# Feed-forward input products, tiles 2 to 10: weights stationary, tokens moving

## The chip, the cores and the metric

The kernel is one program on one core of a Trainium2 chip, one launch. The metric is the device time in microseconds, the median of a few runs; of the kernel before, three runs gave 1437.44 us (1437.07 to 1438.07).

## The reference

Two transformer-like blocks on 256 tokens of width 1024, in float32. The first has a recurrent and an attention branch. The second has two layers; each runs a feed-forward, a mixer, a second feed-forward and a gated embedding. There are thus four feed-forwards, and the change is in them:

```python
def swiglu(x, w_in, w_out):
    gate, up = jnp.split(x @ w_in, 2, axis=-1)
    return (jax.nn.silu(gate) * up) @ w_out

h = h + 0.5 * rmsnorm(swiglu(rmsnorm(h, g[0]), ffn1_w_in[i], ffn1_w_out[i]), g[1])
```

`w_in` is 1024 x 5632 and `w_out` 2816 x 1024. The norm ahead of `swiglu` divides each token by its root mean square; the kernel multiplies by the gains `g[0]` ahead of the products and by the token's scale behind them.

## The kernel before

**Products.** A float32 number is split into a high part, rounded to float32r, and the low part that is left. A product of two matrices is then three products of parts, high x high, high x low and low x high (`three`, lines 2113 to 2116); the product of the low parts is dropped.

**Weights.** All weights of the program are one list of units of 1 MB, 128 x 2048. Four slots hold the raw unit (`raw`), its high part (`whi`) and its low part (`wlo`). SyncE's queue loads a unit as soon as its raw slot is free. ScalarE makes the high part (`hi`, line 422; it waits until TensorE is done with the unit four before), VectorE the low part (`lo`, line 1202). Both work in a fixed order written out by hand for each engine, with their other steps between the units. The counters `n` hold which use of each semaphore is next.

**Tokens.** The 256 tokens are two blocks of 128. The input of a product stands transposed, features on partitions, in `feed_hi` and `feed_lo`. The 2816 features of the feed-forward are 11 tiles of 256; a unit pair holds the 256 gate and the 256 up columns of one tile, for the 1024 rows of depth. Tiles are worked on in pairs, a group of four units: `group_wide` on TensorE takes the tokens' first block through all four units into `acc[0]` and then the second block into `acc[1]`. A feed chunk of 128 x 128 (features x tokens of one block) is stationary and 512 columns of weights move, 12 products for a unit and a block. `acc[t]` is two PSUM banks, one for each tile of the pair. The last tile is alone.

**Behind the products.** When `acc[t]` is complete, ScalarE takes silu of the gate columns, scaled by `pre_rs` (the token's 1/rms, one number for each partition), into `sgl` (line 676), and VectorE multiplies the up columns, `pre_rs` and `sgl` into `hid` and frees `acc[t]` (`mul`, line 1707). Tokens lie on partitions in `hid`, and the output product needs features there, so TensorE turns it: four transposes of 128 x 128 into a bank of `turn` (`hidden`, line 2400, and `turns`, line 2167). ScalarE copies the high part to `hid_hi` (line 683) and VectorE the low part to `hid_lo` (line 1716). Each `hidden` is a hook put into the stream of products of the block after: in the loop, the turn of the pair's second block is done before the last unit of the next group's first block.

**Around the loop.** The first group has hooks of its own: the turn of the normed input's second block, and `hidden(0, 0)` before the third unit of its second block. Then comes a loop of four groups (tiles 2 to 9), tile 10 alone, and the output products in `group_deep` (groups of 3, 4 and 4 units), whose first units carry the last turns. In ScalarE's and VectorE's order, the high and low part of the first group's last slot (unit 7 counted from the start of the feed-forward) come before silu and `mul` of that group's second block.

Of the kernel before, what the change touches and what calls it, by code (L numbers as in the profile page):

```python
# [20 lines left out]
F32 = mybir.dt.float32  # L21
F32R = mybir.dt.float32r
# [4 lines left out]
P = 128  # L27
SEQ, D = 256, 1024
# [16 lines left out]
FF_GROUPS = FF_TILES // 2  # L45
# [69 lines left out]
def build(nc, io):  # L115
    with ExitStack() as ctx:
        def sem(name):
            return ctx.enter_context(nc.semaphore(name))
# [19 lines left out]
        feed_hi = sb("feed_hi", [P, KC, SEQ], F32R)  # L138
        feed_lo = sb("feed_lo", [P, KC, SEQ], F32R)
# [100 lines left out]
        gains2 = sb("gains2", [P, D])  # L240
        assert base[0] <= pp1_at
# [119 lines left out]

        ple_gate, ple_mul, ple_hi, ple_lo = sem("ple_gate"), sem("ple_mul"), sem("ple_hi"), sem("ple_lo")
# [29 lines left out]

        def chunks(ap, n=4):
            return [ap[:, P * i:P * i + P] for i in range(n)]
# [10 lines left out]
        def _(act):  # L405
            n = {"u": 0, "e": [0, 0], "first": 0, "used": 0, "tb": 0, "ss": 0, "h": 0, "ple": 0, "mix": 0, "pre": 0}
# [266 lines left out]
            def ffn(second, layer):  # L673
# [5 lines left out]
                def hidden(g, t, count=4, it=None):  # L679
                    b = next_turn(it)  # L680
                    dst = hid_hi[:, 4 * g:4 * g + count, lanes(t)] if it is None else \
                        hid_hi[:, bass.ds(it * 4 + 4 * g, 4), lanes(t)]
                    act.activation(dst, turn[:, b, 0:P * count].rearrange("p (c s) -> p c s", c=count),  # L683
                                   ACT.Copy).then_inc(fed_hi, 1)

# [33 lines left out]
                hidden(0, 0)  # L719
# [4 lines left out]
                loops = FF_GROUPS - 1  # L724
                start = {k: list(v) if k == "e" else v for k, v in n.items()}
                with act.Fori(0, FF_GROUPS - 1) as it:
                    hidden(0, 1, it=it)
                    silu(0, it)
                    hi(3, it)
                    hidden(1, 0, it=it)  # L730
                    hi(1, it)
                    silu(1, it)
                n.update(u=start["u"] + RING * loops, used=start["used"] + RING * loops,
                         first=start["first"] + loops, tb=start["tb"] + 2 * loops,
                         e=[k + loops for k in start["e"]])

                sums(0)
                act.activation(sgl[:, 0, 0, :], acc[0][:, 0:256], ACT.Silu, scale=pre_rs[:, 0:1]).then_inc(silu_done, 1)
                hi()
                sums(1, units=2)  # L740
                act.activation(sgl[:, 1, 0, :], acc[1][:, 0:256], ACT.Silu, scale=pre_rs[:, 1:2]).then_inc(silu_done, 1)
                hidden(FF_GROUPS - 1, 1)
                hi(3)
                hidden(FF_GROUPS, 0, 2)
                hi()
                hidden(FF_GROUPS, 1, 2)
                if not second and layer == 0:
                    embed(0)
                hi(2 * RING - 4)
# [431 lines left out]
        def _(dve):  # L1181
            n = {"u": 0, "e": [0, 0], "first": 0, "used": 0, "tb": 0, "fed": 0, "rs": 0, "step": 0, "silu": 0,
                 "h": 0, "ple": 0, "post": 0, "pre": 0, "aux": 0, "att": 0}
# [516 lines left out]
            def ffn(second, layer):  # L1700
                def mul(t, it=None, tiles=2, units=RING):

                    no_sums(t, units)
                    n["silu"] += 1
                    dve.wait_ge(silu_done, n["silu"] if it is None else it * 2 + n["silu"])
                    up = acc[t][:, :].rearrange("p (i n) -> p i n", i=2)[:, 0:tiles, 256:512]
                    dve.scalar_tensor_tensor(hid[:, t, 0:tiles, :], up, pre_rs[:, t:t + 1], sgl[:, t, 0:tiles, :],  # L1707
                                             ALU.mult, ALU.mult)\
                        .then_inc(acc_free[t], 1)

                def hidden(g, t, count=4, it=None):
                    b = next_turn(it)
                    n["fed"] += 1
                    dve.wait_ge(fed_hi, n["fed"] if it is None else it * 2 + n["fed"])
                    at = slice(4 * g, 4 * g + count) if it is None else bass.ds(it * 4 + 4 * g, 4)
                    dve.tensor_tensor(hid_lo[:, at, lanes(t)],  # L1716
                                      turn[:, b, 0:P * count].rearrange("p (c s) -> p c s", c=count),
                                      hid_hi[:, at, lanes(t)].bitcast(F32), ALU.subtract).then_inc(moved[b], 1)
# [8 lines left out]
                hidden(0, 0)  # L1727
                lo()
                mul(1)
                loops = FF_GROUPS - 1  # L1730
                start = {k: list(v) if k == "e" else v for k, v in n.items()}
                with dve.Fori(0, loops) as it:
                    hidden(0, 1, it=it)
                    mul(0, it)
                    lo(3, it)
                    hidden(1, 0, it=it)
                    lo(1, it)
                    mul(1, it)
                n.update(u=start["u"] + RING * loops, used=start["used"] + RING * loops,
                         first=start["first"] + loops, tb=start["tb"] + 2 * loops, fed=start["fed"] + 2 * loops,  # L1740
                         silu=start["silu"] + 2 * loops, e=[k + loops for k in start["e"]])
                mul(0, tiles=1)
                lo()
                mul(1, tiles=1, units=2)
                hidden(FF_GROUPS - 1, 1)
                lo()
                lo(2)
                hidden(FF_GROUPS, 0, 2)
                lo()
                hidden(FF_GROUPS, 1, 2)  # L1750
                if not second and layer == 0:
                    embed(0)
                lo(2 * RING - 4)
# [93 lines left out]
            def even():  # L1847
# [6 lines left out]
                assert turns0 % 2 == 0  # L1854
# [249 lines left out]
        def _(pe):  # L2104
            n = {"u": 0, "e": [0, 0], "tb": 0, "h": 0, "dve": 0, "act": 0, "aux": 0, "normed": 0}
# [293 lines left out]
            def ffn(second, layer):  # L2399
                def hidden(g, t, count=4, it=None, back=0):  # L2400

                    pe.wait_ge(acc_free[t], n["e"][t] - back if it is None else it + n["e"][t])
                    turns([hid[:, t, c // 2, P * (c % 2):P * (c % 2) + P] for c in range(count)], it)

                all_moved()
                group_wide(["wide"] * 4, [lambda: feed_normed(xn[:, 1, :]), lambda: hidden(0, 0),
                                          all_moved])
                loops = FF_GROUPS - 1
                start = {k: list(v) if k == "e" else v for k, v in n.items()}
                with pe.Fori(0, loops) as it:  # L2410
                    group_wide(["wide"] * 4, [lambda: hidden(0, 1, it=it), lambda: hidden(1, 0, it=it), None], it)
                n.update(u=start["u"] + RING * loops, tb=start["tb"] + 2 * loops, e=[k + loops for k in start["e"]])
                group_wide(["wide"] * 2, [lambda: None, lambda: hidden(FF_GROUPS - 1, 1, back=1), None])

                hooks = [lambda: hidden(FF_GROUPS, 0, 2, back=1), lambda: hidden(FF_GROUPS, 1, 2, back=1), None]
                group_deep(3, hid_hi, hid_lo, 0, True, False, hooks)
# [423 lines left out]
```

## Time and profile before

| | |
|---|---|
| median of three runs | 1437.44 us |
| the profiled execution | 1437.7 us |
| its span, first to last instruction | 1435.8 us |
| TensorE busy | 1411.9 us, 98% |
| VectorE busy | 874.5 us, 61% |
| ScalarE busy | 710.2 us, 49% |
| mean granted TensorE clock | 0.999 |
| DMA | 272.5 MB, mean 190 GB/s |

Busy time of TensorE counts each matmul from its start to its modelled end, and these overlap, so it says that TensorE always had something in hand and not that it ran at its peak. The time that one instruction costs is read from start to start in the timeline. A line of the program is often that of a helper: L2114, L2115 and L2116 are the three products of `three`, L2167 is the transpose, L422 and L1202 the high and low part of a unit. In the rows, 128x512 is partitions x elements; PE is TensorE, PEld its weight loads, DVE VectorE, ACT ScalarE, POOL GpSimd.

### The profile page before, as it was taken

How to read it: one execution, taken by the hardware profiler on the slowest of the kernel's cores; microseconds unless marked ns; L12 is line 12 of the kernel's file. 1: busy time of each engine (PE TensorE's matmuls, PEld its weight loads, DVE VectorE, ACT ScalarE, POOL GpSimd, SP SyncE). 2: the span in 40 equal slices, each digit the busy share in tenths (PEclk: the TensorE clock that was granted, in tenths of full speed). 3: DMA queues.
4: the chain of work that ended last, by engine and by line, in shares of the span. 5: the costliest groups of instructions: out<-in, count | busy, mean ns of one | idle time of the engine just before them, and what ended most of it. 6: DMA issues, size and time to landing. Idle time of an engine off the chain costs nothing.

```text
span 1435.8 us, 17115 instructions
## 1 busy us (share of the span) xinstructions
PE 1411.9 (98%) x6598; PEld 1168.0 (81%) x6598; DVE 874.5 (61%) x813; ACT 710.2 (49%) x723; POOL 75.4 (5%) x91
## 2 busy tenths in 40 slices
PE   7999999999999999999999999999999999999997
PEld 6888888878888888888888878888888878888886
DVE  6869686775463666774544684544774546554536
ACT  4674766545343557654443554443544445353424
POOL 0000000010000200110000110000202101000001
PEclk9999999999999999999999999999999999999999
DMA  9747554465464453464645374645463633654541
GB/s 393 296 150 264 179 178 168 164 243 207 172 217 163 179 210 118 147 226 155 234 176 196 142 263 148 234 176 203 155 228 118 221 131 139 228 188 163 201 181 44
DMA packets 40380, 272.51 MB, mean 190 GB/s; under 512 B 4609, under 2 KB 5505, under 8 KB 8706
## 3 DMA queue, kind: packets, MB, share of 16 engines
q1 hardware_dynamic: 36864, 261.65, 50.2%
q10 hardware_dynamic: 3458, 10.04, 2.0%
q8 instruction: 42, 0.69, 0.2%
q14 instruction: 16, 0.13, 0.0%
HBM read 270.62 MB, written 1.05 MB: 189 GB/s over the span
## 4 chain that ended last, share of the span: by engine, by line
PE 91%; DVE 4%; DMA 3%; ACT 1%; issue 1%; POOL 1%; SPq 0%; ACTq 0%; DVEq 0%; POOLq 0%
PE acc L2114 28%; PE acc L2116 28%; PE acc L2115 28%; PE turn L2167 4%; DVE wlo L1202 2%; DMA raw<-in_units 2%; DMA mod_raw<-in_units 1%; PE aux L2654 0%; PE turn L2316 0%; PE aux L2528 0%; DMA gpost<-in_g_final 0%; DVE h L1272 0%; ACT whi L422 0%; DVE xn L1256 0%; DVE mod_part L1321 0%
## 5 line engine op out<-in xcount | busy, mean ns | idle before, releaser
L1202 DVE TENSOR_TENSOR wlo<-raw,whi 128x2048 fp32r<-128x2048 f32 x233 | 533.1, 2297 | 257.4 <-ACT whi L422 257.3
L2114 PE MATMUL acc<-whi,feed_hi 128*128 128x512 f32 (+1 forms) x1496 | 595.1, 398 | 4.2 <-DVE wlo L1202 4.2
L2116 PE MATMUL acc<-whi,feed_lo 128*128 128x512 f32 (+1 forms) x1496 | 582.6, 389 | 0.0
L2115 PE MATMUL acc<-wlo,feed_hi 128*128 128x512 f32 (+1 forms) x1496 | 581.9, 389 | 0.0
L422 ACT ACTIVATE whi<-raw 128x2048 fp32r<-128x2048 f32 x233 | 445.3, 1917 | 255.8 <-PE acc L2116 243.5
L2114 PEld LDWEIGHTS acc<-whi,feed_hi 128*128 128x128 f32 x1496 | 281.7, 188 | 65.1 <-DVE wlo L1202 6.5
L2116 PEld LDWEIGHTS acc<-whi,feed_lo 128*128 128x128 f32 x1496 | 281.3, 188 | 59.6
L2115 PEld LDWEIGHTS acc<-wlo,feed_hi 128*128 128x128 f32 x1496 | 281.8, 188 | 55.7 <-issue 1.2
L2114 PE MATMUL acc<-whi,hid_hi 128*128 128x512 f32 x352 | 138.0, 392 | 0.0
L2116 PE MATMUL acc<-whi,hid_lo 128*128 128x512 f32 x352 | 137.1, 389 | 0.0
L2115 PE MATMUL acc<-wlo,hid_hi 128*128 128x512 f32 x352 | 137.0, 389 | 0.0
L2116 PEld LDWEIGHTS acc<-whi,hid_lo 128*128 128x128 f32 x352 | 66.1, 188 | 13.7
L2115 PEld LDWEIGHTS acc<-wlo,hid_hi 128*128 128x128 f32 x352 | 66.1, 188 | 13.4
L2114 PEld LDWEIGHTS acc<-whi,hid_hi 128*128 128x128 f32 x352 | 66.1, 188 | 13.3
L683 ACT ACTIVATE hid_hi<-turn 128x512 f32 (+2 forms) x48 | 26.4, 550 | 99.3 <-PE turn L2167 99.3
L1716 DVE TENSOR_TENSOR hid_lo<-turn,hid_hi 128x512 f32 (+2 forms) x48 | 30.8, 642 | 71.8 <-ACT hid_hi L683 71.8
L1102 POOL TENSOR_SCALAR ms<-ss 128x1 f32<-128x1 f32 x18 | 12.2, 680 | 1033.7 <-ACT xn L442 1011.4
L1707 DVE SCALAR_TENSOR_TENSOR hid<-acc,pre_rs,sgl 128x512 f32<-128x512 f32 (+1 forms) x48 | 33.8, 704 | 44.0 <-ACT sgl L676 40.1
L464 ACT ACTIVATE feed_hi<-turn 128x512 fp32r<-128x512 f32 x48 | 26.2, 594 | 56.4 <-PE turn L2167 56.4
L1240 DVE TENSOR_TENSOR feed_lo<-turn,feed_hi 128x512 fp32r<-128x512 f32 x48 | 30.9, 684 | 30.7 <-ACT feed_hi L464 30.7
L676 ACT ACTIVATE sgl<-acc,pre_rs 128x512 f32<-128x512 f32 x40 | 27.2, 679 | 37.1 <-PE acc L2116 37.1
L1265 DVE SCALAR_TENSOR_TENSOR xn<-acc,gpost 128x1024 f32<-128x1024 f32 x12 | 14.6, 1221 | 38.4 <-ACT xn L442 38.4
(338 smaller groups left out, 879.7 us busy)
## 6 DMA issues: line engine op xcount, KB each, us to landing
raw<-in_units SPq DMA_DIRECT2D x237, 1024.0 KB, 4.9
mod_raw<-in_units SPq DMA_DIRECT2D x6, 1024.0 KB, 11.2
gpost<-in_norm_g ACTq DMA_DIRECT2D x8, 512.0 KB, 4.8
gpre<-in_norm_g ACTq DMA_DIRECT2D x6, 512.0 KB, 5.7
mod_more<-in_units SPq DMA_DIRECT2D x2, 1024.0 KB, 23.5
h<-in_x SPq DMA_DIRECT2D x2, 512.0 KB, 10.6
w_ax<-in_w_ax SPq DMA_DIRECT2D x1, 1024.0 KB, 26.2
bgate<-in_b_gate SPq DMA_DIRECT2D x1, 1024.0 KB, 27.5
```

The source lines that it names most:

```text
L422: act.activation(whi[:, u % RING, :], raw[:, u % RING, :], ACT.Copy).then_inc(hi_ready, 1)
L464: act.activation(dst[:, 4 * i:4 * i + 4, lanes(t)], turn[:, b, :].rearrange("p (c s) -> p c s", c=4), ACT.Copy).then_inc(fed_hi, 1)
L676: act.activation(sgl[:, t, :, :], acc[t][:, :].rearrange("p (i n) -> p i n", i=2)[:, :, 0:256], ACT.Silu, scale=pre_rs[:, t:t + 1]).then_i ...
L683: act.activation(dst, turn[:, b, 0:P * count].rearrange("p (c s) -> p c s", c=count), ACT.Copy).then_inc(fed_hi, 1)
L1202: dve.tensor_tensor(wlo[:, u % RING, :], raw[:, u % RING, :], whi[:, u % RING, :].bitcast(F32), ALU.subtract).then_inc(lo_ready, 1)
L1240: dve.tensor_tensor(dst[part], turn[:, b, :].rearrange("p (c s) -> p c s", c=4), hi_part[part].bitcast(F32), ALU.subtract).then_inc(moved[ ...
L1707: dve.scalar_tensor_tensor(hid[:, t, 0:tiles, :], up, pre_rs[:, t:t + 1], sgl[:, t, 0:tiles, :], ALU.mult, ALU.mult)\
L1716: dve.tensor_tensor(hid_lo[:, at, lanes(t)], turn[:, b, 0:P * count].rearrange("p (c s) -> p c s", c=count), hid_hi[:, at, lanes(t)].bitca ...
L2114: pe.matmul(out, xh, wh, start=first, stop=False)
L2115: pe.matmul(out, xh, wl, start=False, stop=False)
L2116: return pe.matmul(out, xl, wh, start=False, stop=last)
L2167: last = pe.transpose(turn[:, b, P * i:P * i + P], part, ident[:, :])
```

## The change

Tiles 0 and 1 stay as they were. For tiles 2 to 10 the roles are exchanged: a block of 128 x 128 weights is stationary and the tokens move. `feed_hi` and `feed_lo` are now two halves of one tensor `feeds`, so that one matmul of 512 columns takes the high weights through both, and one of 256 columns takes the low weights through the high feed. The result has 128 features on partitions and, for each of two banks (0 gate, 1 up), high-feed sums in the columns 0 to 255 and low-feed sums in 256 to 511. `acc[c]` holds the feature block c of the tile; it gets two units of products, and not four.

The two halves of a bank are added by two engines: ScalarE copies the second half to `sgl` (`tile_rest`), VectorE adds the first (`tile_sum`) and frees `acc[c]`. The token scale now differs along the free dimension, so it is turned once for each feed-forward into a row `rs_row` that stands on all partitions (`rows_scale` on TensorE, a copy on VectorE), and VectorE multiplies all four sums by it (`tile_scale`). ScalarE takes silu, VectorE the product, ScalarE the high part and VectorE the low part, all in SBUF. There are no transposes for these tiles; `hid_split` counts them for TensorE ahead of the output products. `hidden(1)`, the turn of the first group's second block, now stands between the first and second unit of tile 2's block c = 0. The program runs tile 2, a loop of 3 x 2 tiles, and tiles 9 and 10.

```diff
@@ allocation @@
-        feed_hi = sb("feed_hi", [P, KC, SEQ], F32R)
-        feed_lo = sb("feed_lo", [P, KC, SEQ], F32R)
+        feeds = sb("feeds", [P, 2, KC, SEQ], F32R)
+        feed_hi, feed_lo = feeds[:, 0, :, :], feeds[:, 1, :, :]
...
+        rs_row = sb("rs_row", [P, SEQ])
@@ ScalarE @@
+                def tile_gate(it=None):
+                    n["scaled"] += 1
+                    act.wait_ge(gate_scaled, n["scaled"] if it is None else it * 2 + n["scaled"])
+                    act.activation(sgl[:, :, 0, :], sgl[:, :, 0, :], ACT.Silu).then_inc(silu_done, 1)
+
+                def tile_rest(c, it=None):
...
+                    both = acc[c][:, :].rearrange("p (i x n) -> p i x n", i=2, x=2)
+                    act.activation(sgl[:, c, :, :], both[:, :, 1, :], ACT.Copy).then_inc(rest_copied, 1)
+
+                def tile_hi(j, it=None):
...
+                    act.activation(hid_hi[:, at, :], hid[:, :, 0, :], ACT.Copy).then_inc(fed_hi, 1)
+
+                def tile_done(j, it=None):
+                    hi(1, it)
+                    tile_rest(1, it)
+                    hi(1, it)
+                    tile_gate(it)
+                    tile_hi(j, it)
+                    if j < FF_LAST:
+                        tile_rest(0, it)
...
                 hi(3)
-                hidden(0, 0)
+                n["tb"] += 1
+                hidden(0)
                 hi()
                 if late:
                     pre_scale(1)
                 silu(1)
...
+                hidden(1)
+                tile_rest(0)
+                tile_done(FF_FIRST)
...
+                with act.Fori(0, FF_LOOPS) as it:
+                    for j in (FF_FIRST + 1, FF_FIRST + 2):
+                        tile_done(j, it)
@@ VectorE @@
+                def tile_sum(c, it=None):
...
+                    dve.tensor_tensor(sgl[:, c, :, :], both[:, :, 0, :], sgl[:, c, :, :], ALU.add).then_inc(acc_free[c], 1)
+
+                def tile_scale(it=None):
+
+                    for c in range(2):
+                        dve.wait_ge(acc_free[c], n["e"][c] if it is None else it * 2 + n["e"][c])
+                    rows = sgl[:, :, :, :].rearrange("p t i n -> p (t i) n")
+                    dve.tensor_tensor(rows, rows, rs_row[:, :].rearrange("p (o n) -> p o n", o=1)
+                                      .to_broadcast([P, 4, SEQ]), ALU.mult).then_inc(gate_scaled, 1)
+
+                def tile_product(it=None):
...
+                    dve.tensor_tensor(hid[:, :, 0, :], sgl[:, :, 0, :], sgl[:, :, 1, :], ALU.mult).then_inc(hid_made, 1)
+                    n["made"] += 1
+                    dve.wait_ge(hid_made, n["made"] if it is None else it * 2 + n["made"])
+
+                def tile_lo(j, it=None):
...
+                    dve.tensor_tensor(hid_lo[:, at, :], hid[:, :, 0, :], hid_hi[:, at, :].bitcast(F32), ALU.subtract)\
+                        .then_inc(hid_split, 1)
+
+                def tile_done(j, it=None):
+                    tile_sum(1, it)
+                    tile_scale(it)
+                    lo(1, it)
+                    tile_product(it)
+                    if j < FF_LAST:
+                        tile_sum(0, it)
+                    tile_lo(j, it)
+                    lo(1, it)
...
                 mul(0)
                 lo(3)
-                hidden(0, 0)
+                row_moved = take(rs_row[:, :], columns=SEQ, groups=1)
+                hidden(0)
                 lo()
                 mul(1)
...
+                hidden(1)
+                dve.wait_ge(moved[row_moved[0]], row_moved[1])
+                tile_sum(0)
+                tile_done(FF_FIRST)
@@ TensorE @@
+                def hidden(t):
+
+                    pe.wait_ge(acc_free[t], n["e"][t])
+                    turns([hid[:, t, c // 2, P * (c % 2):P * (c % 2) + P] for c in range(4)])
+
+                def rows_scale():
+                    pe.wait_ge(pre_rstd, TOK * ((1, 3), (4, 6))[layer][1 if second else 0])
+                    turns([pre_rs[:, t:t + 1].to_broadcast([P, P]) for t in range(TOK)])
+
+                def turned_unit(u, half, c):
+
+                    s = u % RING
+                    for b in range(2):
+                        both = acc[c][:, BANK * b:BANK * b + BANK]
+                        for k in range(4):
+                            kc, at = 4 * half + k, BANK * k + SEQ * b + P * c
+                            w = slice(at, at + P)
+                            pe.matmul(both, whi[:, s, w], feeds[:, :, kc, :], start=kc == 0, stop=False)
+                            ins = pe.matmul(both[:, 0:SEQ], wlo[:, s, w], feed_hi[:, kc, :], start=False, stop=kc == KC - 1)
+                    return ins
+
+                def tile(it=None, hook=None):
+
+                    u0 = n["u"]
+                    n["u"] += 2
+                    for c in range(2):
+                        ready(c, None if it is None else it * 2)
+                        for half in range(2):
+                            if half and not c and hook is not None:
+                                hook()
+                            unit(u0 + half, c, it)
+                            ends(turned_unit(u0 + half, half, c), c, half == 1)
...
+                def second_hook():
+                    rows_scale()
+                    hidden(0)
+
+                group_wide(["wide"] * 4, [lambda: feed_normed(xn[:, 1, :]), second_hook, all_moved])
+                tile(hook=lambda: hidden(1))
+                tile()
...
+                with pe.Fori(0, FF_LOOPS) as it:
+                    for _ in range(2):
+                        tile(it)
...
+                tile()
+
+                all_moved()
...
+                pe.wait_ge(hid_split, split0 + 7 - FF_FIRST)
+                group_deep(3, hid_hi, hid_lo, 0, True, False, [None, None, None])
                 group_deep(4, hid_hi, hid_lo, 6, False, False, [None, None, None])
-                all_moved()
+                pe.wait_ge(hid_split, n["split"])
```

## Rows read from the trace of the kernel before

**Rows 1.** The page: busy time by engine, then the chain that ended last.
```profile
PE 1411.9 (98%) x6598; PEld 1168.0 (81%) x6598; DVE 874.5 (61%) x813; ACT 710.2 (49%) x723; POOL 75.4 (5%) x91
...
PE 91%; DVE 4%; DMA 3%; ACT 1%; issue 1%; POOL 1%; SPq 0%; ACTq 0%; DVEq 0%; POOLq 0%
PE acc L2114 28%; PE acc L2116 28%; PE acc L2115 28%; PE turn L2167 4%; DVE wlo L1202 2%; DMA raw<-in_units 2%; DMA mod_raw<-in_units 1%; PE aux L2654 0%; PE turn L2316 0%; PE aux L2528 0%; DMA gpost<-in_g_final 0%; DVE h L1272 0%; ACT whi L422 0%; DVE xn L1256 0%; DVE mod_part L1321 0%
```

**Rows 2.** Timeline inside a feed-forward (start, us, engine, line, operation): products, one turn.
```profile
700.13 0.39 PE L2116 MATMUL acc<-whi,feed_lo 128*128 128x512 f32 x1
...
702.85 0.39 PE L2116 MATMUL acc<-whi,feed_lo 128*128 128x512 f32 x1
...
703.09 0.60 PE L2167 MATMUL turn<-setup,hid 128*128 128x128 f32 x4
...
703.44 0.48 PE L2114 MATMUL acc<-whi,feed_hi 128*128 128x512 f32 x1
...
703.75 0.40 PE L2115 MATMUL acc<-wlo,feed_hi 128*128 128x512 f32 x1
```

**Rows 3.** Timeline of TensorE, third feed-forward: group 2, first output product, a small turn.
```profile
855.49 0.39 PE L2114 MATMUL acc<-whi,feed_hi 128*128 128x512 f32 x1
...
957.78 0.39 PE L2114 MATMUL acc<-whi,hid_hi 128*128 128x512 f32 x1
...
962.99 0.39 PE L2116 MATMUL acc<-whi,hid_lo 128*128 128x512 f32 x1
...
963.67 0.39 PE L2115 MATMUL acc<-wlo,hid_hi 128*128 128x512 f32 x1
```

**Rows 4.** Timeline of TensorE in the even mixer: first and last of 24 narrow products.
```profile
504.10 0.28 PE L2114 MATMUL acc<-whi,feed_hi 128*128 128x256 f32 x1
...
506.85 0.28 PE L2116 MATMUL acc<-whi,feed_lo 128*128 128x256 f32 x1
```

**Rows 5.** Timeline of VectorE, then of ScalarE, where the third feed-forward enters group 2.
```profile
854.98 2.29 DVE L1202 TENSOR_TENSOR wlo<-raw,whi 128x2048 fp32r<-128x2048 f32 x1 [0.92 <-ACT whi L422]
...
857.19 0.68 DVE L1716 TENSOR_TENSOR hid_lo<-turn,hid_hi 128x512 fp32r<-128x512 f32 x1
857.79 2.28 DVE L1202 TENSOR_TENSOR wlo<-raw,whi 128x2048 fp32r<-128x2048 f32 x1
859.99 0.74 DVE L1707 SCALAR_TENSOR_TENSOR hid<-acc,pre_rs,sgl 128x512 f32<-128x512 f32 x1
...
855.75 1.92 ACT L422 ACTIVATE whi<-raw 128x2048 fp32r<-128x2048 f32 x1 [0.32 <-PE acc L2116]
```

**Rows 6.** Timeline where a turn waits for VectorE, before the third feed-forward.
```profile
825.12 0.69 DVE L1256 TENSOR_TENSOR xn<-h,gpre 128x512 f32<-128x512 f32 x1
...
825.87 0.66 PE L2167 MATMUL turn<-setup,xn 128*128 128x128 f32 x4 [0.73 <-DVE xn L1256]
...
826.28 0.48 PE L2114 MATMUL acc<-whi,feed_hi 128*128 128x512 f32 x1
...
826.60 0.40 PE L2115 MATMUL acc<-wlo,feed_hi 128*128 128x512 f32 x1
```

**Rows 7.** Groups by line and shape, whole run: busy, mean ns, idle before.
```profile
L1240 DVE TENSOR_TENSOR feed_lo<-turn,feed_hi 128x512 fp32r<-128x512 f32 x48 | 30.9, 684 | 30.7 <-ACT feed_hi L464 30.7
...
L1716 DVE TENSOR_TENSOR hid_lo<-turn,hid_hi 128x256 fp32r<-128x256 f32 x8 | 3.3, 418 | 0.0
...
L1779 DVE TENSOR_TENSOR xn<-xn,pp 128x1024 f32<-128x1024 f32 x2 | 2.4, 1222 | 2.7 <-ACT xn L781 2.7
...
L676 ACT ACTIVATE sgl<-acc,pre_rs 128x512 f32<-128x512 f32 x40 | 27.2, 679 | 37.1 <-PE acc L2116 37.1
...
L524 ACT ACTIVATE xn<-acc 128x512 f32<-128x512 f32 x4 | 2.4, 590 | 5.2 <-PE acc L2116 5.2
```

**Rows 8.** Stretches: us, busy time of five engines, granted clock, DMA.
```profile
14.00:18.00 4.00, 1.09 (x6) 0.69 (x5) 3.89 (x5) 1.15 (x2) 0.09 (x1) 1.00 1.01 420
...
1434.00:1436.00 2.00, 0.00 (x0) 0.00 (x0) 0.00 (x0) 0.00 (x0) 0.00 (x0) 0.50 0.46 170
```

More of the change, by code:

```diff
@@ L1700, in ffn, with mul @@
             def ffn(second, layer):
-                def mul(t, it=None, tiles=2, units=RING):
-                    no_sums(t, units)
+                def mul(t):
+                    no_sums(t)
+                    n["silu"] += 1
+                    dve.wait_ge(silu_done, n["silu"])
+                    up = by_two(acc[t][:, :])[:, :, 256:512]
+                    dve.scalar_tensor_tensor(hid[:, t, :, :], up, pre_rs[:, t:t + 1], sgl[:, t, :, :],
+                                             ALU.mult, ALU.mult)\
+                        .then_inc(acc_free[t], 1)
@@ new lines, in hidden @@
+                def hidden(t):
+                    b = next_turn()
+                    n["fed"] += 1
+                    dve.wait_ge(fed_hi, n["fed"])
+                    dve.tensor_tensor(hid_lo[:, 0:4, lanes(t)], turn[:, b, :].rearrange("p (c s) -> p c s", c=4),
+                                      hid_hi[:, 0:4, lanes(t)].bitcast(F32), ALU.subtract).then_inc(moved[b], 1)
+                def tile_sum(c, it=None):
+                    no_sums(c, 2)
+                    both = acc[c][:, :].rearrange("p (i x n) -> p i x n", i=2, x=2)
+                    n["rest"] += 1
+                    dve.wait_ge(rest_copied, n["rest"] if it is None else it * 4 + n["rest"])
+                    dve.tensor_tensor(sgl[:, c, :, :], both[:, :, 0, :], sgl[:, c, :, :], ALU.add).then_inc(acc_free[c], 1)
@@ L1726, in ffn @@
                 lo(3)
-                hidden(0, 0)
+                row_moved = take(rs_row[:, :], columns=SEQ, groups=1)
+                hidden(0)
                 lo()
                 mul(1)
-                loops = FF_GROUPS - 1
+                hidden(1)
+                dve.wait_ge(moved[row_moved[0]], row_moved[1])
+                tile_sum(0)
+                tile_done(FF_FIRST)
                 start = {k: list(v) if k == "e" else v for k, v in n.items()}
[L1732 to L1750, printed above, removed]
+                with dve.Fori(0, FF_LOOPS) as it:
+                    for j in (FF_FIRST + 1, FF_FIRST + 2):
+                        tile_done(j, it)
+                n.update(u=start["u"] + RING * FF_LOOPS, used=start["used"] + RING * FF_LOOPS,
+                         first=start["first"] + 2 * FF_LOOPS, fed=start["fed"] + 2 * FF_LOOPS,
+                         silu=start["silu"] + 2 * FF_LOOPS, e=[k + 2 * FF_LOOPS for k in start["e"]],
+                         made=start["made"] + 2 * FF_LOOPS, rest=start["rest"] + 4 * FF_LOOPS)
+                tile_done(FF_LAST - 1)
+                tile_done(FF_LAST)
+                lo(3)
                 if not second and layer == 0:
                     embed(0)
-                lo(2 * RING - 4)
+                lo()
+                lo(3)
                 for t in range(TOK):
```

88 lines of the change are left out of this document (35 added, 53 removed).

## The prediction

> **What bounds the kernel now.** I read the page first: TensorE is busy 98% of the span, the chain that ended last is 91% TensorE, and the lines of the weight products (28% each) carry it [rows 1]. A busy TensorE row proves little, since each matmul record lasts 0.39 us while the next starts 0.227 us later, so I went to the timeline and read start to start. Twelve steps from 700.13 to 702.85 give 0.2267 us for a matmul of 512 columns, and nothing stands between them: in this stage TensorE streams without a wait, and an edit is worth what it changes in the number and width of TensorE's instructions, plus any wait that it creates. All four feed-forwards have the same steps, so I work one out and take it four times. In the third, the second group (feature tiles 2 and 3) starts at 855.49 and the first product of the output matrix at 957.78: 102.29 us for tiles 2 to 10 [rows 3].
>
> **Price of a turn.** Four transposes between products: from the product at 702.85 to the third after it (703.75) are 0.90 us, less two steps of 0.2267, so 0.447 us [rows 2]. A turn of two: 962.99 to 963.67 is 0.68, less 0.453, so 0.227 us [rows 3].
>
> **Width.** In the 256-column products of the even mixer, 23 steps take 506.85 - 504.10 = 2.75 us, so 0.1196 each [rows 4]. That is 0.1071 less than at 512 columns, which is 256 columns at 2.4 GHz; what is left of either step (0.2267 - 0.2133, 0.1196 - 0.1067) is a fixed 13 ns per product. Every product here loads its own weights, at both widths, so the load is already inside the step.
>
> **Products, removed and added.** A tile before: 2 blocks of tokens x 8 chunks of depth x 3 products x 512 columns = 48 steps. After: 4 feature blocks x 8 chunks x (one of 512, both feeds together, and one of 256) = 32 + 32 steps. The columns are the same, 24,576; there are 16 more instructions at 13 ns, +0.21 us a tile. With the units' edges included: 102.29 less 9 full turns (4.02) over 4x96 + 48 = 432 products is 0.2275 us a step, and 0.2275 - 0.1071 = 0.1204 for the narrow one. Nine tiles: 288 x 0.2275 + 288 x 0.1204 = 65.5 + 34.7 = 100.2 us.
> The moving operand is now two runs of 256 from two feeds. No row shows such a read. Below, it costs nothing (one run of 512 [rows 2]); above, what two separate products cost more than one, 2 x 0.1196 - 0.2267 = 0.0125 us each, 1152 of them, 14.4 us. I take nothing, since the number of columns streamed is the same; the upper end stays for the range.
> The Trainium skill (TensorE: Matmul & The Clock Gate, "Back-to-back issue gap") puts a single gap at N/2.4 plus 2.5 ns. By it the 16 extra products of a tile would cost 0.04 us and not 0.21, and the sum for four feed-forwards would be 6 us lower. Rows 2 and 4 disagree, with 13 ns at both widths; the measurement decides.
>
> **Turns, removed and added.** After 855.49 the old code has 9 full turns and 2 small ones (those fall into the first output products). The new one has one full turn, `hidden(1)`, and one of two transposes, the scale row, directly ahead of the turn of `hidden(0)`; next to another turn it costs about the difference between full and small spread over two transposes more, (0.447 - 0.227)/4 x 2 = 0.11; with a wait of its own I take 0.14 us.
>
> **The new wait.** `hidden(1)` stood before the last unit of the next block, 36 products or 8.2 us into group 2. It now stands after the first half of tile 2's first block: 8 x (0.2275 + 0.1204) = 2.78 us after 855.49. It waits for `acc_free[1]`, that is for VectorE's `mul(1)`, which VectorE does only after the low part of unit 7. That unit's slot comes free when the group ends: ScalarE starts its copy at 855.75, VectorE subtracts from 857.79, and `mul(1)` runs from 859.99 to 860.73 = 5.24 us after the group's start [rows 5]. Before, this was 3 us early; now it is late. In front of it VectorE gets one more instruction, the copy of the scale row out of PSUM, 128x256, 0.42 us by the 128x256 row [rows 7]: the feed part (857.19) shifts to about 857.53, unit 7 from 857.79 to 858.13, so `mul(1)` ends 0.34 later, at 5.58. A turn released by VectorE starts 0.06 us after it (825.12 + 0.69 = 825.81, turn at 825.87) and then takes 0.41 + 0.32 instead of 0.35 + 0.31 to the second product, 0.07 more [rows 6]. Stall: 5.64 - 2.78 + 0.07 = 2.9 us. Behind the turn in TensorE's queue wait all products of tile 2, so nothing hides it. Bounds: 2.6 (the copy fits into a gap) to 3.6 us (a wait's hand-over of 0.3 twice). The copies of ScalarE and VectorE are one tile ahead of need, so nothing is won back.
>
> **Is the rest covered?** Per tile of 32 x 0.3479 = 11.13 us, by durations of [rows 5, 7] and counted from the end of a tile's second block: ScalarE copies half of `acc[1]` 0.26 to 0.85, VectorE adds to 1.57, scales (128x1024, 1.22) to 2.85, low part of the next unit to 5.1, product to 5.8; ScalarE the high part of hid to 6.4, the copy from `acc[0]` to 7.0; VectorE its sum to 7.7, low part of hid 8.4, second unit 10.7. TensorE needs `acc[1]` at 5.5 (has it at 1.6) and `acc[0]` at 11.1 (7.7); VectorE is through 1.3 us ahead of its next sum (12.0). VectorE does 2 x 0.68 + 1.22 + 2 x 0.69 [rows 6] + 2 x 2.29 = 8.5 of 11.1 us. The edit costs nothing there as long as this slack lasts. Loads: the number and order of units is the same; SyncE's queue sees the slots come free singly and not in threes.
> The thinnest place is the entry to the output matrix: its third unit is needed after 24 steps, 5.46 us, and has its low part at 5.1. Cover 0.3 us; I take no stall, and 0.3 us x 4 as the upper end.
>
> **Sum.** One feed-forward before: 102.29 + 2 x 0.227 = 102.74. After: 100.18 + 0.45 + 0.14 + 2.9 = 103.7. Difference +0.95, of which the turns give -4.0, the extra instructions +1.9, the copy of the scale row's turn +0.14 and the stall +2.9. Four times: +3.8 us. The profiled execution took 1437.7 us (span 1435.8), which gives 1441.5; from the median of 1437.44 it is 1441.2 us.
>
> **Rivals.**
> *No stall, faster.* If the wait at half a tile is met in time, the turns removed win: 4 x (0.95 - 2.9) = -7.8, 1429.6 us. For it: the turns are worth 4 us in each feed-forward. Against: the chain 0.26 + 1.92 + 2.29 + 0.74 after the group's end is all serial and its records [rows 5] end at 5.24; it decides at 2.78. Chance 0.10, which includes a lower fixed cost of a product than I read.
> *Clock.* TensorE has no record for about 2.8 us in each stall. In the stretch 14 to 18 us it sat idle 2.9 us at a granted clock of 1.00; after the last product the clock is 0.50 [rows 8]. If it fell to 1.2 GHz for as long as the stall, 2.9 us of work would take twice that: 4 x 2.9/2 = +5.8, 1447 us. Chance 0.10. The Trainium skill (same page, "Why this matters for your kernels") warns against idle gaps between bursts for this reason; the nearest row has a gap of this size without it.
> *Vector chain late.* If VectorE's tile takes longer than 11.13 (waits for its own results, the in-place sum in strided halves), each tile is late by the excess: 0.3 us x 36 = +10.8, 1452 us. For it: five hand-overs a tile between two engines, four more than before. Against: 1.3 us of slack. Chance 0.10.
> *Narrow products cost more.* If a weight load of 0.19 us were exposed under a 256-column product, 1152 x 0.07 = +80, 1518 us. The even mixer's rows [rows 4] are exactly such products at 0.1196. Chance 0.03; a few ns for the split read fall into the range instead.
>
> **How the numbers follow.** The forecast holds 0.67 by itself. A change under 0.2% (2.9 us) can't be told from none. The forecast's +3.8 lies 0.9 above that; with its own scatter of about 1.5 us a quarter of it, 0.17, lies within. Slower 0.50 + 0.10 + 0.10 + 0.03 = 0.73; same 0.17; faster 0.10. The range runs from 1437.6 (stall at its lower end and half the extra instructions free) to 1450 (the clock case, and most of a late vector chain or of the split read).
>
> **What would show it.** After: no turn between products from tile 3 on; steps of 0.227 and 0.120 in turn; a tile period of 11.1 us; one gap ahead of the turn in tile 2 of each feed-forward, released by VectorE's `mul`, 2.9 us long; output products starting 103.5 us after tile 2 does; no wait at `acc_free` or a unit's low part elsewhere; granted clock 1.00. Wrong if that gap is missing or shorter than 2 us, if a pair of steps isn't 0.347, or if gaps recur tile by tile.

## The result and the profile after

The changed kernel takes 1448.54 us (median of 5 runs, 1447.81 to 1451.84) against 1437.31: ratio 1.0083, 95% interval 1.0072 to 1.0095. It is slower by 11.2 us, where +3.8 was forecast; the time lies inside the range of 1437.6 to 1450 and on the side that was forecast, but the size was a third of what came. The profiled execution took 1447.81 us, its span is 1446.0, 10.2 us over the span before.

The page of the changed kernel; the first two lines answer to [rows 1], the others are the new products (busy, mean ns).

```profile
PE 1412.0 (98%) x7038; PEld 1187.3 (82%) x7038; DVE 959.4 (66%) x917; ACT 748.6 (52%) x787; POOL 75.2 (5%) x91
...
PE 89%; DVE 6%; DMA 2%; ACT 2%; issue 1%; POOL 1%; SPq 0%; ACTq 0%; DVEq 0%; POOLq 0%
...
L2484 PE MATMUL acc<-feeds,whi 128*128 128x512 f32 x1152 | 406.5, 397 | 0.0
...
L2485 PE MATMUL acc<-feeds,wlo 128*128 128x256 f32 x1152 | 323.9, 281 | 0.0
```

TensorE is as busy as before by the page, and its busy time is the same; neither tells of the 10 us. VectorE's share of the chain rose from 4 to 6%, since the chain now runs through VectorE's work ahead of each new wait. The timeline shows the wait. VectorE, then TensorE, in the third feed-forward, where tile 2 starts at 859.76 (this answers to [rows 5]):

```profile
861.46 0.42 DVE L1262 COPY rs_row<-turn 128x256 f32<-128x256 f32 x1
861.79 0.68 DVE L1748 TENSOR_TENSOR hid_lo<-turn,hid_hi 128x512 fp32r<-128x512 f32 x1
862.39 2.28 DVE L1235 TENSOR_TENSOR wlo<-raw,whi 128x2048 fp32r<-128x2048 f32 x1
864.59 0.75 DVE L1740 SCALAR_TENSOR_TENSOR hid<-acc,pre_rs,sgl 128x512 f32<-128x512 f32 x1
...
862.45 0.28 PE L2485 MATMUL acc<-feeds,wlo 128*128 128x256 f32 x1
865.39 0.66 PE L2234 MATMUL turn<-setup,hid 128*128 128x128 f32 x4 [2.66 <-DVE hid L1740]
865.80 0.48 PE L2484 MATMUL acc<-feeds,whi 128*128 128x512 f32 x1
...
867.04 0.63 PE L2484 MATMUL acc<-feeds,whi 128*128 128x512 f32 x1
867.47 0.41 PE L2485 MATMUL acc<-feeds,wlo 128*128 128x256 f32 x1
867.68 0.63 PE L2484 MATMUL acc<-feeds,whi 128*128 128x512 f32 x1
```

`mul(1)` ends at 865.34, 5.58 us after the tile's start, to the hundredth as worked out. The last product before the turn starts at 862.45 and the turn at 865.39, 2.94 us later in place of 0.12: the stall. Behind it the products first go on at their old step, and then take 0.43 and 0.21 us in place of 0.23 and 0.12. The stretches of the same trace (us, five engines, granted clock, DMA) say why:

```profile
862.60:865.30 2.70, 0.13 (x2) 0.00 (x0) 2.70 (x2) 0.00 (x0) 0.00 (x0) 1.00 0.87 309
865.30:870.30 5.00, 4.91 (x21) 4.29 (x22) 0.73 (x2) 0.60 (x1) 0.00 (x0) 0.66 0.66 256
870.30:875.30 5.00, 5.00 (x30) 4.35 (x30) 0.69 (x1) 2.51 (x2) 0.00 (x0) 1.00 0.00 0
```

The mean of 0.66 is a mixture of the two levels: behind the stall the clock was at 1.2 GHz for a part of these 5 us, while TensorE worked through them. The same happened at all four stalls of this execution, and the granted clock of the five runs (0.994, 0.994, 0.994, 0.996 and 0.995, against 0.998 to 0.999 of the kernel before) says that none of them was free of it.

There is a third thing, in no view by groups. Eleven products of 512 columns and ten of 256, in the first and in the third feed-forward, far from any stall and at a granted clock of 1.00:

```profile
350.20 0.39 PE L2484 MATMUL acc<-feeds,whi 128*128 128x512 f32 x1
...
353.67 0.39 PE L2484 MATMUL acc<-feeds,whi 128*128 128x512 f32 x1
...
880.12 0.40 PE L2484 MATMUL acc<-feeds,whi 128*128 128x512 f32 x1
...
883.65 0.40 PE L2484 MATMUL acc<-feeds,whi 128*128 128x512 f32 x1
```

A pair is one wide product and the narrow one behind it. Ten pairs take 3.47 us in the one and 3.53 in the other. Over the last 256 pairs the mean is 0.3467 us in three feed-forwards and 0.3533 in the third, without exception inside a feed-forward: behind the stall and the lowered clock it is in one step or the other to its end. Ahead of the turn all four are alike, at 0.351 (seven pairs from 859.76 to 862.22). The 288 pairs of nine tiles take 99.8 or 101.75 us.

The account by feed-forward, from tile 2's start to the first output product (before: 102.29, and two small turns of 0.227 behind it, so 102.74):

| | measured | pairs | turn, stall | left: lower clock |
|---|---|---|---|---|
| first | 104.47 | 99.84 | 3.35 | 1.3 |
| second | 104.59 | 99.84 | 3.35 | 1.4 |
| third | 106.57 | 101.75 | 3.35 | 1.5 |
| fourth | 104.65 | 99.84 | 3.35 | 1.5 |

The last column is what the other two leave of the measured time. The sum is 420.3 against 411.0, +9.3. The first group, which now holds the turn of the scale row, takes 0.17, 0.21, 0.20 and 0.24 us more than before, +0.8 (worked out: 0.6), and 0.1 is spread over the rest.

### The profile page after: what moved, and what is told of

It is laid out like the page before. It is cut to its first block, busy times and chain, and to the rows that moved or that the text cites. A ratio compares the mean times of both kernels' runs of the same rounds, so it can differ in the third digit from the quotient of the medians.

```text
span 1446.0 us, 18169 instructions
## 1 busy us (share of the span) xinstructions
PE 1412.0 (98%) x7038; PEld 1187.3 (82%) x7038; DVE 959.4 (66%) x917; ACT 748.6 (52%) x787; POOL 75.2 (5%) x91
## 4 chain that ended last, share of the span: by engine, by line
PE 89%; DVE 6%; DMA 2%; ACT 2%; issue 1%; POOL 1%; SPq 0%; ACTq 0%; DVEq 0%; POOLq 0%
PE acc L2181 18%; PE acc L2484 18%; PE acc L2183 18%; PE acc L2182 18%; PE acc L2485 9%; DVE wlo L1235 3%; PE turn L2234 3%; ACT whi L431 1%; DMA mod_raw<-in_units 1%; DMA gpost<-in_norm_g 1%; PE aux L2758 0%; PE turn L2383 0%; PE aux L2309 0%; PE aux L2632 0%; DMA gpost<-in_g_final 0%
## 5 line engine op out<-in xcount | busy, mean ns | idle before, releaser
L2484 PE MATMUL acc<-feeds,whi 128*128 128x512 f32 x1152 | 406.5, 397 | 0.0
L2181 PE MATMUL acc<-whi,feeds 128*128 128x512 f32 (+1 forms) x888 | 354.5, 399 | 4.2 <-DVE wlo L1235 4.2
L2183 PE MATMUL acc<-whi,feeds 128*128 128x512 f32 (+1 forms) x888 | 345.8, 389 | 0.0
L2182 PE MATMUL acc<-wlo,feeds 128*128 128x512 f32 (+1 forms) x888 | 345.2, 389 | 0.0
L2485 PE MATMUL acc<-feeds,wlo 128*128 128x256 f32 x1152 | 323.9, 281 | 0.0
L2484 PEld LDWEIGHTS acc<-feeds,whi 128*128 128x128 f32 x1152 | 218.3, 190 | 50.4
L2485 PEld LDWEIGHTS acc<-feeds,wlo 128*128 128x128 f32 x1152 | 219.5, 191 | 0.2
L2181 PEld LDWEIGHTS acc<-whi,feeds 128*128 128x128 f32 x888 | 167.6, 189 | 41.9 <-DVE wlo L1235 6.8
L2183 PEld LDWEIGHTS acc<-whi,feeds 128*128 128x128 f32 x888 | 167.3, 188 | 35.4
L2182 PEld LDWEIGHTS acc<-wlo,feeds 128*128 128x128 f32 x888 | 167.7, 189 | 32.8 <-issue 0.7
L1757 DVE TENSOR_TENSOR sgl<-acc,sgl 128x512 f32<-128x512 f32 x72 | 49.8, 692 | 122.4 <-ACT sgl L708 122.4
L708 ACT ACTIVATE sgl<-acc 128x512 f32<-128x512 f32 x72 | 42.5, 590 | 43.5 <-PE acc L2485 43.5
```

The lines of the kernel that those rows point to most:

```text
L708: act.activation(sgl[:, c, :, :], both[:, :, 1, :], ACT.Copy).then_inc(rest_copied, 1)
L1757: dve.tensor_tensor(sgl[:, c, :, :], both[:, :, 0, :], sgl[:, c, :, :], ALU.add).then_inc(acc_free[c], 1)
L2181: pe.matmul(out, xh, wh, start=first, stop=False)
L2182: pe.matmul(out, xh, wl, start=False, stop=False)
L2183: return pe.matmul(out, xl, wh, start=False, stop=last)
L2484: pe.matmul(both, whi[:, s, w], feeds[:, :, kc, :], start=kc == 0, stop=False)
```

## Experiments

Each is timed against the kernel before on the same chip, 1437.3 us in the first two sets and 1437.5 in the last. "The nine tiles" is the time from tile 2 to the first output product.

**e1_hook_late.** The turn later; `hidden(1)` behind `tile_rest(0)` and `tile_sum(0)` on the other engines.

```diff
-                            if half and not c and hook is not None:
+                            if half and c and hook is not None:
...
-                tile(hook=lambda: hidden(1))
+                tile(hook=lambda: hidden(1, back=1))
```

> The changed kernel, with one turn moved: hidden(1) stands before the last half of tile 2's second block, 8.3 us into the tile and not 2.8, by when VectorE's mul has freed the bank (5.6 us). ScalarE's and VectorE's work on the tile's first block goes ahead of their part of the turn. Theory (the stall and the clock that falls behind it are the whole loss): no gap and granted clock 1.00; per feed-forward -4.03 us of turns, +1.57 us for the 16 more products a tile (9 tiles, 0.3467 us a pair as measured), +0.2 for the scale row's turn: 4 x -2.3 = -9 us against before, about 1428. Rival (the products themselves are dearer, the stall was hidden elsewhere): 1437 or more. If the gap goes but the clock still falls: about 1434.

Measured: 1436.09 us, ratio 0.9989 (0.9980 to 0.9999). No gap, clock 1.00, nine tiles in 102.24, 102.23, 102.24 and 102.22 us. The stall and the fallen clock are gone and the time is 12.4 us less; but all four feed-forwards run at 0.3533 us a pair, which is 7.6 us over an expectation that had taken 0.3467 for all. The theory was right about what the stall costs and wrong that nothing else was left.

**e2_mul_early.** The same end by the other side of the wait.

```diff
-                hi()
                 if late:
                     pre_scale(1)
                 silu(1)
+                hi()
 ...
                 lo(3)
+                mul(1)
                 row_moved = take(rs_row[:, :], columns=SEQ, groups=1)
                 hidden(0)
                 lo()
-                mul(1)
```

> The changed kernel with the turn where the change put it, but silu(1) and mul(1) put ahead of the high and low part of unit 7, in ScalarE's and VectorE's order. Theory: mul(1) ends 2.5 us after tile 2's start and the turn is asked for at 2.78, so the gap closes to under 0.3 us and the clock stays: about 1428 us, as with the later turn. Rival (the gap is set by another wait, such as the buffer of the turn): the gap stays at 2.8 us and the time at 1448. Second rival (moving the low part of unit 7 back by 0.75 us makes TensorE wait for it in tile 3): a new wait on L1235, 1430 or more.

Measured: 1436.39 us (1432.61 to 1436.96, 10 runs), ratio 0.9991 (0.9982 to 1.0001). The gap is gone. Timeline where it was, VectorE's `mul` and TensorE's turn, which starts 0.22 us after the last product:

```profile
334.47 0.75 DVE L1740 SCALAR_TENSOR_TENSOR hid<-acc,pre_rs,sgl 128x512 f32<-128x512 f32 x1
...
335.47 0.28 PE L2485 MATMUL acc<-feeds,wlo 128*128 128x256 f32 x1
...
335.69 0.63 PE L2234 MATMUL turn<-setup,hid 128*128 128x128 f32 x4
```

The time is 8 us over the 1428 that was expected. No new wait on unit 7 appears. The nine tiles take 102.32, 100.46, 102.32 and 100.47 us: two feed-forwards in the slow step and two in the fast. That profile is of the fastest run; the others lie at 1434.5, 1434.9, 1435.3 and 1436.2 to 1437.0, which fits up to two slow steps (1.9 us each) above; their granted clock is the same, 0.998 to 0.999. So one kernel changes its step from run to run: this is read from the times, since only one run has a trace.

**e3_fill_stall.** Work in the stall.

```diff
+                def filled():
...
+                    for _ in range(11):
+                        pe.matmul(turn[:, b, :], feed_hi[:, 0, 0:P], feeds[:, :, 0, :], start=True, stop=True)
+                    hidden(1)
...
+                tile(hook=filled)
```

> The changed kernel, with 11 matmuls of 512 columns put into each stall, ahead of the wait; their sums go to the buffer of the turn and are overwritten by it. The wait is as long, but TensorE works 2.5 of its 2.8 us. Theory (the clock falls because TensorE is idle in the stall): the turn starts at the same time after tile 2's start (5.6 us), granted clock 1.00 behind it, and 1.3 to 1.5 us less in each feed-forward than in the changed kernel, 5.7 us or more in all: 1441 to 1443. Rival (the slow steps behind the stall come from the layout or from the restart): they stay, 1448.

Measured: 1447.19 us (1445.33 to 1447.50, 4 runs). The timeline around the first stall: the turn comes when VectorE is done, as ever, and behind it stand steps of 0.31 and 0.12, not 0.58 and 0.21.

```profile
335.48 2.72 PE L2511 MATMUL turn<-feeds 128*128 128x512 f32 x11
...
338.30 0.66 PE L2234 MATMUL turn<-setup,hid 128*128 128x128 f32 x4
...
338.72 0.48 PE L2484 MATMUL acc<-feeds,whi 128*128 128x512 f32 x1
...
339.03 0.28 PE L2485 MATMUL acc<-feeds,wlo 128*128 128x256 f32 x1
...
339.15 0.40 PE L2484 MATMUL acc<-feeds,whi 128*128 128x512 f32 x1
```

The clock was 1.00 behind all four. The time missed the forecast because all four feed-forwards are at 0.3533: 101.75 + 0.45 + 2.9 = 105.1, measured 105.06 each. What the clock gave back (5.6 us) the step took (5.7 us, three more slow ones). A trace without a fall could be luck, as e7's below; but the other three runs show 0.998 to 0.999 as well, so of 16 filled stalls few or none had a fall, against 0.994 to 0.996 in every run of the changed kernel. Without the trace this run would have spoken against the right cause.

**e4_before_early_hook.** The kernel before, with the wait at the wrong place.

```diff
+                if it is not None and t == 0:
+                    return i == 1
```

> The kernel before, without the change, but in its loop the turn of a pair's second block stands before the second unit of the next group and not before the fourth, 2.73 us after the group's start. VectorE's mul ends 5.24 us after it. 16 stalls in all. Theory (wait alone): each is 5.24 + 0.06 - 2.73 + 0.07 = 2.6 us, +42 us, 1479.6. With the clock falling behind each as in the changed kernel (1.3 to 1.7 us): +63 to +70, 1500 to 1507. Rival (the clock falls for what is special in the changed kernel): 1480.

Measured: 1498.54 us, +61.2. There are 16 gaps of 2.82 to 2.89 us between starts. Behind 12 of them the clock fell, each time at a loss of about 1.6 us, and behind 4 not. Two gaps of the same length, one with and one without:

```profile
365.38 0.66 PE L2167 MATMUL turn<-setup,hid 128*128 128x128 f32 x4 [2.44 <-DVE hid L1707]
...
366.81 0.63 PE L2115 MATMUL acc<-wlo,feed_hi 128*128 128x512 f32 x1
367.23 0.63 PE L2116 MATMUL acc<-whi,feed_lo 128*128 128x512 f32 x1
...
392.37 0.65 PE L2167 MATMUL turn<-setup,hid 128*128 128x128 f32 x4 [2.44 <-DVE hid L1707]
...
393.56 0.39 PE L2114 MATMUL acc<-whi,feed_hi 128*128 128x512 f32 x1
393.79 0.39 PE L2115 MATMUL acc<-wlo,feed_hi 128*128 128x512 f32 x1
```

16 x 2.67 + 12 x 1.6 = 61.9, where the nine tiles of the four feed-forwards are longer by 62.0. So both prices belong to the wait, not to the new layout, and the layout before had them as well once its hook asked too early. The Trainium skill (TensorE: Matmul & The Clock Gate, "Why this matters for your kernels") advises against idle gaps between bursts of matmuls, naming longer ones than these. The traces agree in kind, with a fall behind 12 of 16 gaps here and at 4 of 4 in the changed kernel, and show that it is not certain: 4 of 16 went without one here, and all 4 in e7's trace below.

**e5_grouped_early, e7_grouped_only.** Four wide products and then four narrow ones, without and with the stall.

```diff
                         for k in range(4):
                             ...
                             pe.matmul(both, whi[:, s, w], feeds[:, :, kc, :], start=kc == 0, stop=False)
+                        for k in range(4):
+                            ...
                             ins = pe.matmul(both[:, 0:SEQ], wlo[:, s, w], feed_hi[:, kc, :], start=False, stop=kc == KC - 1)
```

> As e2_mul_early (no stall), and in each bank the four products of 512 columns of a unit come first and then the four of 256, in place of wide and narrow in turn. The same 64 products a tile. In the runs so far a pair in turn takes 0.3467 us in some feed-forwards and 0.3533 in others, 1.9 us for each that is in the slow step. Theory (the two steps come from wide and narrow in turn): eight products take 4 x 0.2267 + 4 x 0.1196 = 1.385 us in every feed-forward, and the time is that of e2 with no slow one, 1428 to 1430 us, with less spread than e2's 4 us. Rival (the slow step comes from the weights as stationary operand or from the two feeds read as one operand): the spread stays and the median is 1436.

Measured: 1433.34 us (1433.00 to 1434.12, 8 runs), ratio 0.9973 (0.9962 to 0.9983); nine tiles in 101.62, 101.62, 101.61 and 101.61 us. The timeline, two rounds of a bank:

```profile
701.12 1.09 PE L2484 MATMUL acc<-feeds,whi 128*128 128x512 f32 x4
702.05 0.64 PE L2488 MATMUL acc<-feeds,wlo 128*128 128x256 f32 x4
702.52 1.09 PE L2484 MATMUL acc<-feeds,whi 128*128 128x512 f32 x4
```

Over the last 256 pairs, eight products take 1.403 us, 0.3508 a pair, and not the 1.385 that I had added up, which is why the time is 3 us over the expected range. The steps of 0.3467 and 0.3533 are gone, the spread with them (1.1 us for 4.4), so it is the alternation that lets them lie 1.9 us a feed-forward apart; the level is between the two.

> The changed kernel with its stall, and the grouped order of e5_grouped_early. Theory: stall of 2.9 us and fallen clock stay (1.3 to 1.7 us a feed-forward), the slow step goes: per feed-forward 99.8 + 0.45 + 2.9 + 1.4 = 104.5, against 104.5 to 106.6 in the changed kernel, so 1445.5 to 1447 us with little spread, against 1447.8 to 1451.8. Rival: the spread and the median of 1448.5 stay.

Measured: 1446.79 us (1444.60 to 1450.52, 4 runs). The spread stayed, against what I expected, but it is now of the clock alone. The profiled execution is the fastest, and in it the clock fell behind none of four stalls (nine tiles: 104.33 to 104.36, where 101.0 + 0.45 + 2.9 = 104.4). The runs of 1444.60, 1445.71, 1447.87 and 1450.52 us have granted clocks of 0.999, 0.998, 0.996 and 0.994: the time grows as the clock falls, and the slowest, 5.9 us or four times 1.5 longer, has the clock of the changed kernel with four falls. The same order of products with the same stall thus has anything from no fall to about four.

**e6_feeds_adjacent, e9_flip_every_chunk.** Two more tries at the step.

```diff
-        feeds = sb("feeds", [P, 2, KC, SEQ], F32R)
+        feeds = sb("feeds", [P, KC, 2, SEQ], F32R)
...
-                            pe.matmul(both, whi[:, s, w], feeds[:, :, kc, :], start=kc == 0, stop=False)
+                            pe.matmul(both, whi[:, s, w], feeds[:, kc, :, :], start=kc == 0, stop=False)
```

> As e2_mul_early, but the two feeds of a depth chunk lie side by side in SBUF, so that the moving operand of 512 columns is one run and not two of 256. Theory (the split read costs nothing and has no part in the two steps): both steps again, 0.3467 and 0.3533, median 1432 to 1437. Rival (the split read makes the slow step): 0.3467 everywhere, 1428 to 1429.

Measured: 1436.05 us (1432.80 to 1437.34, 10 runs), ratio 0.9987. One run of 512 is no better than two of 256: the profile has 102.31 or 102.32 in all four, the runs spread as e2's do. The split read costs nothing that shows: its slow step is e2's (102.32).

```diff
-                        for k in range(4):
+                        for k, low in ((0, 0), (0, 1), (1, 1), (1, 0), (2, 0), (2, 1), (3, 0), (3, 1)):
...
```

> As e2_mul_early, but the order of the two products flips from chunk to chunk: wide, narrow, narrow, wide and so on (and narrow, wide at the last two), so that alternation is mostly broken into twos. Measured so far: strict alternation 0.3467 or 0.3533 us a pair from one feed-forward to the next, groups of four 0.350 always. Theory (two steps only where wide and narrow strictly alternate): one step between these everywhere, 101 to 102 us for a feed-forward's nine tiles, a median of 1431 to 1436 with a spread under 1 us. Rival (the step is fixed by how the stream started, at the turn): two values again, a spread of several us.

Measured: 1436.54 us (1435.81 to 1437.24, 10 runs), ratio 0.9993. One value, as the theory says, but it missed the value: 0.3533 a pair and 102.28 to 102.31 us everywhere, the slow step and not one between, a median 0.5 us above the expected range and a spread of 1.4 us and not under 1.

**e8_half_fill.** As e3 with 5 matmuls.

> As e3_fill_stall with 5 matmuls in the place of 11: TensorE works the first 1.1 us of each stall and then has 1.7 us without work. Theory (the clock falls only after idling about as long as the whole stall): granted clock 1.00 behind all four, a time as e3_fill_stall's, 1441 to 1447 by the pair steps. Rival (a gap of 1.7 us is enough): steps of 0.43 and 0.21 us behind some of them, 1.3 us each.

Measured: 1447.15 us in one run. A gap of 1.49 us is left before each turn, and the clock stayed at 1.00 behind all four; all four are in the slow step, 105.05 to 105.07 us. One execution shows no more than that.

```profile
335.71 1.33 PE L2511 MATMUL turn<-feeds 128*128 128x512 f32 x5
...
338.53 0.66 PE L2234 MATMUL turn<-setup,hid 128*128 128x128 f32 x4 [1.49 <-DVE hid L1740]
```

**e10_late_grouped.** e1's turn and e5's order.

> The later turn of e1_hook_late with the grouped order of e5_grouped_early. In e1_hook_late all four feed-forwards ran at 0.3533 us a pair. Theory: the grouped order gives 0.350 wherever the turn stands, so 101.6 us for each feed-forward's nine tiles, 0.6 us less than e1_hook_late in each, and the time is e5's, 1433.3. Rival (the late turn leaves the stream in a slow state whatever the order): 1436.

Measured: 1432.91 us (1432.37 to 1434.17, 9 runs), ratio 0.9969 (0.9959 to 0.9979); nine tiles in 101.37 to 101.57 us. The grouped order is without the large steps wherever the turn stands, but it is not one value either: 0.3500 a pair in three feed-forwards and 0.3508, e5's, in the second, which is 0.2 us a feed-forward. This is the best version: 4.6 us under the kernel before, 15.6 under the changed one. Its account: 4 x (101.42 - 102.74) + 0.6 = -4.7.

## Why the prediction was right or wrong

- *TensorE is the bound, steps read from start to start.* Right. In every run the sum of steps and gaps gives the nine tiles to within 0.4 us.
- *Turns, -4.0 us a feed-forward.* Right, as far as it can be seen: with the stall away, e1's nine tiles are 288 x 0.3533 + 0.45 = 102.2, measured 102.24, with nothing in the place of the turns.
- *Extra products, +1.9 us.* Half right. For the fast step (0.3467 a pair) it was 0.3 us too high, for the slow one (0.3533) 1.6 us too low. I had one step for each width from streams of one width and took their mixture for the sum; the mixture has steps of its own. That is 1.9 us for each slow feed-forward, one in the profiled execution. The two slowest runs are 3.7 and 4.0 us above it at the same granted clock (0.994), so more falls of the clock don't explain them; two more slow feed-forwards would, but this is not shown, since they have no trace.
- *The new wait, 2.9 us.* Right in place, cause and size: `mul(1)` at 5.58 us, gap 2.82 us and 0.1 for the restart. Moving either side of it (e1, e2) removes it.
- *The rest is covered.* Right, but for the scale row's turn, +0.2 us a feed-forward and not 0.14. No wait of TensorE in the tiles or at the entry to the output products.
- *The clock.* This is the term that failed. The sum left it at zero, and it was 5.6 us; as a rival it stood there with its mechanism, at +5.8 us, and with a chance of 0.10. And the row that it leaned on, 14 to 18 us [rows 8], was misread. It prints 1.00 ahead of and behind the idle gap, but so does the stretch from 26 to 29 us, where the products stand 0.43 us apart, the step of the lower level, until about 29 us; only then do they stand 0.23 apart. Four transposes ahead of the gap take 1.12 us there, where others take 0.66 [rows 6]. Kernel before, TensorE and one stretch:

```profile
13.71 1.12 PE L2167 MATMUL turn<-setup,xn 128*128 128x128 f32 x4
17.74 3.58 PE L2242 MATMUL aux<-ones,mod_part 128*128 128x1 f32 x16 [2.91 <-DVE mod_part L1324]
...
26.76 0.63 PE L2114 MATMUL acc<-whi,feed_hi 128*128 128x512 f32 x1
27.19 0.63 PE L2115 MATMUL acc<-wlo,feed_hi 128*128 128x512 f32 x1
...
29.54 0.40 PE L2115 MATMUL acc<-wlo,feed_hi 128*128 128x512 f32 x1
29.77 0.40 PE L2116 MATMUL acc<-whi,feed_lo 128*128 128x512 f32 x1
...
26.00:29.00 3.00, 3.00 (x9) 2.32 (x8) 2.71 (x3) 1.96 (x2) 0.00 (x0) 1.00 1.02 423
```

So the printed clock can't be trusted in the first 29 us, and by these rows TensorE was at 1.2 GHz already on both sides of that gap: it was no case of a gap without a fall. Real ones exist, four among the 16 of e4 and four in e7's trace, but the changed kernel's five runs and e4 say that a fall is the likelier outcome. The rival's size, 1.45 us a stall against 1.3 to 1.5 measured, is partly luck: it let the clock be low for just as long as the stall, and in the third feed-forward it fell only some 1.4 us after the turn began (866.8).
- *Sum.* Forecast +3.8; clock +5.6, one slow step +1.9, pairs otherwise -1.4, scale row and rest 0.3: +10.2, the difference of the spans.
- *Rivals.* "No stall, faster" would have been 1429.6 by my numbers; e1, e2, e5 and e10 are that case and reach 1432.9 to 1436.4, by the pair step alone. The vector chain was never late, and narrow products cost no exposed load (that rival's 1518 was counted from the time before; from the forecast it is 1522).
- *Range and signs.* By the terms named for it, the lower end of the range is 1441.2 - 1.2 - 3.7, about 1436, not 1437.6. Of the signs, the gap, its releaser and its length came as written. Two failed, as the terms above did: the granted clock was not 1.00 throughout, and in one feed-forward the pair was not 0.347. Tile 2 to the first output product took 104.5 to 106.6 us and not 103.5.

Left open: what makes the clock fall behind one gap and not behind the next of the same length; what makes a feed-forward go on in the fast or the slow step; and whether some order gives 0.3467 always, which by this account would be about 1429 us.

## What to carry to other kernels

A hook that asks for another engine's result has a latest good time and an earliest one; when the work between hooks is halved in length, work out anew when its producer is done, counted from the event that starts that chain. Price a stall of the matrix engine of two to three microseconds at more than its length, since the clock may fall behind it, at some 1.5 us each here. Read the clock from the step of equal products beside the printed value. And a stream of matmuls of two widths in turn is to be measured as such, and over several executions: it may have more than one steady step.

## What the runs showed of the hardware

- A matmul with weights of its own takes 13 ns over its columns at 2.4 GHz, at 512 and 256 columns [rows 2, 4]. Wide and narrow strictly in turn take 0.3467 or 0.3533 us a pair, steady to the end of a feed-forward, both within one execution of the changed kernel and of e2. The two are 6.7 ns apart, which is 16 periods of 2.4 GHz. In fours a pair takes 0.3500 or 0.3508 (e5, e7, e10), in flipped twos 0.3533 (e9).
- Equal gaps of TensorE (2.44 to 2.50 us without a record) left the granted clock alone 4 times of 16 and lowered it 12 times, with a loss of about 1.6 us each (e4). Gaps of 2.94 to 2.97 us from start to start came with a fall 4 times of 4 in the changed kernel's trace (1.3 to 1.5 us each) and 0 times of 4 in e7's. With TensorE at work in the gap, or in half of it, there was none (e3's and e8's traces, 0 of 4 each).
- The printed clock of the first 29 us is 1.00 while the products stand 0.43 us apart (kernel before): there, the steps tell the level.
- A moving operand of two runs of 256 streams as fast as one run of 512 (e6).
